# A two-layer transformer kernel: the MLP products by quarters with seven products in place of eight, and modulation weights summed along rows by VectorE

## What is computed

```python
h = modulate(rms_norm(x, mlp_norm[layer]), sh_m, sc_m)        # h * (1 + sc) + sh
x = x + gt_m * squared_relu_mlp(h, mlp_w1[layer], mlp_w2[layer])

def squared_relu_mlp(h, w1, w2):                              # w1: 1024 x 4096, w2: 4096 x 1024
    return jnp.square(jax.nn.relu(h @ w1)) @ w2

c_act = jax.nn.silu(c)                                        # 1024 values
mod = (c_act @ ada_w[layer] + ada_b[layer])                   # 1024 x 6144; kv_ada_w: 1024 x 2048
```

## Time and profile before

| | us |
|---|---|
| median of 3 runs | 2585.69 |
| lowest, highest | 2585.17, 2588.85 |
| the profiled execution | 2587.35 |
| its span, first to last instruction | 2585.6 |

### The profile page before, as it was taken

How to read it: one execution, slowest core, us unless ns; L and a number is a source line. 1 busy time by engine, 2 the same in 40 slices (tenths; PEclk the granted TensorE clock), 3 DMA queues, 4 the chain that set the end, 5 groups by cost and what they waited for, 6 DMA issues and landing times. The chain is left out here.

```text
span 2585.6 us, 22377 instructions
## 1 busy us (share of the span) xinstructions
PE 2444.9 (95%) x8264; PEld 1216.3 (47%) x8264; DVE 823.2 (32%) x1835; ACT 465.4 (18%) x995; POOL 42.9 (2%) x50
## 2 busy tenths in 40 slices
PE   6999899999999999989999999999999899998886
PEld 4444544444444645554444444464554643343332
DVE  4444432112122436653211213138642411110104
ACT  2232211110000324441211100021231200000001
POOL 0000000000000000000000000000000000000000
PEclk9999799999999999989999999999999899999998
DMA  8443213333433111112433433341003569999995
GB/s 341 158 168 147 98 65 130 130 130 130 169 157 130 57 65 50 49 74 98 163 130 132 172 151 130 130 163 65 33 1 130 230 266 427 426 426 425 424 422 205
DMA packets 45426, 452.29 MB, mean 175 GB/s; under 512 B 7784, under 2 KB 7784, under 8 KB 20240
## 3 DMA queue, kind: packets, MB, share of 16 engines
q1 hardware_dynamic: 37616, 435.64, 42.0%
q0 software_dynamic: 6528, 12.17, 1.3%
q10 hardware_dynamic: 1184, 3.19, 0.3%
HBM read 444.54 MB, written 18.39 MB: 179 GB/s over the span
## 5 line engine op out<-in xcount | busy, mean ns | idle before, releaser
L959 PE MATMUL ps<-big,ring 128*128 128x512 f32 x1024 | 448.9, 596 | 3.9 <-PEq L871 1.8
L901 PE MATMUL ps<-hT,ring 128*128 128x512 f32 x1024 | 444.3, 594 | 0.0
L959 PEld LDWEIGHTS ps<-big,ring 128*128 128x128 f32 x1024 | 192.6, 191 | 245.9 <-issue 245.9
L901 PEld LDWEIGHTS ps<-hT,ring 128*128 128x128 f32 x1024 | 193.9, 191 | 237.9 <-issue 236.6
L2572 PE MATMUL ps<-ring,big 128*64 128x512 f32 (+1 forms) x768 | 233.3, 614 | 25.2 <-issue 15.3
L512 PE MATMUL ps<-hT,ring 128*128 128x512 f32 x384 | 175.0, 607 | 2.1 <-ACT hT L429 2.1
L2572 PEld LDWEIGHTS ps<-ring,big 128*64 128x64 f32 (+1 forms) x768 | 85.2, 151 | 144.3 <-issue 131.0
L1653 PE MATMUL ps<-hT,ring 128*128 128x512 f32 x320 | 142.4, 600 | 2.7 <-DVE big L2035 1.7
L2572 PE MATMUL ps<-big 128*64 128x512 f32 (+1 forms) x352 | 130.0, 604 | 6.6 <-ACT big L2633 3.3
L207 DVE SCALAR_TENSOR_TENSOR tmp<-ring,cact,tmp 128x512 f32<-128x512 f32 (+1 forms) x192 | 131.6, 685 | 6.8
L856 DVE TENSOR_TENSOR mod<-ps,vec 128x4 f32 (+1 forms) x16 | 2.6, 162 | 367.4 <-PE ps L214 367.4
(11 more groups left out here) (433 smaller groups left out, 2506.6 us busy)
## 6 DMA issues: line engine op xcount, KB each, us to landing
ring<-in_stream SPq DMA_DIRECT2D x99, 2048.0 KB, 8.4
ring<-in_gate SPq DMA_DIRECT2D x17, 2048.0 KB, 29.2
ring<-in_up SPq DMA_DIRECT2D x16, 2048.0 KB, 25.2
ring<-in_down SPq DMA_DIRECT2D x15, 2048.0 KB, 27.4
big<-in_up SPq DMA_DIRECT2D x9, 2048.0 KB, 25.2
big<-in_down SPq DMA_DIRECT2D x8, 2048.0 KB, 27.1
big<-in_gate SPq DMA_DIRECT2D x7, 2048.0 KB, 24.8
hT<-in_down SPq DMA_DIRECT2D x5, 2048.0 KB, 26.5
```

What stands on the lines that cost most here:

```text
L901: last = pe.matmul(m.ps[:, j, :], w[:, k, j * P:(j + 1) * P], m.hT[:, k, :], start=(k == 0), stop=(k == KT - 1))
L959: last = pe.matmul(m.ps[:, bank(half, j), :], w[:, k, j * P:(j + 1) * P], hid[:, 8 * c + k, :], start=(c == 0 and k == 0), stop=(c == 3 an ...
```

## The change

**Products.** Rows and columns are split in half, and four products of quarters with their sums are made from seven products P1 to P7 (Strassen's scheme in Winograd's form). In the first product chunk 0 stays as it was; each of the other seven chunks is done in two pairs `(c, q)`. A pair makes four 128 x 256 quarters of hidden tiles f = 4c + q and g = 4c + 2 + q. The inner dimension is split into k = 0 to 3 and 4 to 7, so each P is 4 matmuls of 256 columns into its own bank (line L919 of the changed kernel). The sums of weight quarters (`sums_a`, `sums_b`) are made by VectorE ahead of the pair, those of `hT` (`t1`, `t2`, `t4`) once. VectorE joins the seven banks (`u2`, `u4`, `u3`, `c22`, `c11`, `c21`, `c12`), and ScalarE copies P1 out and applies ReLU and Square to each quarter. In the second product a step `s` is one `k` of one chunk with its partner `4 + k`: 32 steps (16 for each half of the output), each 7 products of 2 matmuls of 256 columns (L1108), accumulated over the 16 steps in seven banks. VectorE makes the weight sums and the sums of hidden quarters per step (`sums`: 8 additions of 256 in the first half, 7 in the second, where one sum of hidden quarters is left in place by the first half). `outputs` joins the banks after a half's last step and `joined` scales and adds to `xT` by quarters, so tiles come in the order 2, 3, 0, 1.

**Modulation.** The weights are laid out with outputs on partitions (`output_rows`, on the host, where the other weights are laid out too). The activated condition vector is spread over all partitions once per MLP (8 matmuls with the identity in place of 7 that kept TensorE busy, then a copy by ScalarE to `crow`). Each 128 outputs are one instruction over 1024 elements with an accumulator (L869), four (three in the second MLP) per chunk. The row sums by TensorE are gone. The first product's loop is unrolled.

TensorE, first product, the end of a chunk before, and the first pair and the beginning of the second after. `relu`, `h_ok`, `mm` are semaphores; L906 gives the slot back.

The diff, cut to the parts that the prediction speaks of:

```diff
+    def modulation(dve, n, j0, j1, o, done, total):
+        slot = n % RING
+        if j0 == 0:
+            dve.wait_ge(m.full[slot], 16 * (n // RING + 1))
+        for j in range(j0, min(j1, tiles)):
+            w = m.ring[:, slot, j * D:(j + 1) * D]
+            dve.scalar_tensor_tensor(w, w, 1.0, crow, ALU.mult, ALU.mult, accum_out=mod_out[:, o + j:o + j + 1]).then_inc(done, 1)
+        if j1 == 4:
+            dve.wait_ge(done, total)
+            dve.sem_inc(m.free[slot], 1)
...
+    bank = dict(P1=0, P6=1, P5=2, P7=3, P2=4, P4=5, P3=6)
+    b11, b12, b21, b22 = m.hT[:, 0:4, 0:H], m.hT[:, 0:4, H:T], m.hT[:, 4:8, 0:H], m.hT[:, 4:8, H:T]
+    pairs = [(c, q) for c in range(1, 8) for q in range(2)]
...
+                def product(name, a, b):
+                    out = m.ps[:, bank[name], 0:H]
+                    for k in range(4):
+                        ins = pe.matmul(out, a[:, k, :], b[:, k, :], start=(k == 0), stop=(k == 3))
+                    ins.then_inc(prod, 1)
...
+                pe.wait_ge(t_ok, 1)
+                pe.wait_ge(relu, 4)
+                pe.wait_ge(cond_ok, 1)
+                for i, (c, q) in enumerate(pairs):
+                    if q == 0:
+                        pe.wait_ge(m.full[chunk1(c)[0]], chunk1(c)[1])
+                    a11, a12, a21, a22 = quarters(c, q)
+                    if i:
+                        pe.wait_ge(p1_ok, i)
+                    product("P1", a11, b11)
+                    pe.wait_ge(s12_ok, i + 1)
+                    if i:
+                        pe.wait_ge(u2_ok, i)
+                    product("P6", s2, t2)
+                    if i:
+                        pe.wait_ge(u4_ok, i)
+                        pe.wait_ge(c22, i)
+                    product("P5", s1, t1)
+                    if i:
+                        pe.wait_ge(u3_ok, i)
+                    pe.wait_ge(s3_ok, i + 1)
+                    pe.wait_ge(t3_ok, 1)
+                    product("P7", a21, b12)
...
+                    product("P4", a22, t4)
+                    if i:
+                        pe.wait_ge(c12, i)
+                    pe.wait_ge(s4_ok, i + 1)
+                    product("P3", s4, b22)
+                    if q == 1:
+                        pe.wait_ge(prod, PRODUCTS * (i + 1))
+                        pe.sem_inc(m.free[chunk1(c)[0]], 1)
...
+                def sums_a(c, q):
+                    a11, a12, a21, a22 = quarters(c, q)
+                    if q == 0:
+                        dve.wait_ge(m.full[chunk1(c)[0]], chunk1(c)[1])
+                    c1.link(dve.tensor_tensor(s1, a21, a22, ALU.add))
+                    dve.tensor_tensor(s2, s1, a11, ALU.subtract).then_inc(s12_ok, 1)
+                    dve.tensor_tensor(a21, a11, a21, ALU.subtract).then_inc(s3_ok, 1)
+                def sums_b(c, q, i):
+                    dve.wait_ge(s12_ok, i + 1)
+                    dve.tensor_tensor(s4, quarters(c, q)[1], s2, ALU.subtract).then_inc(s4_ok, 1)
+                def ada(c, j0, j1):
+                    modulation(dve, at + 2 * c + 1, j0, j1, tiles * c, mod_done, tiles * (c + 1))
...
+                for i, (c, q) in enumerate(pairs):
+                    f, g = 4 * c + q, 4 * c + 2 + q
+                    ps = lambda name: m.ps[:, bank[name], 0:H]
+                    done = PRODUCTS * i
+                    dve.wait_ge(p1_ok, i + 1)
+                    dve.wait_ge(prod, done + 2)
+                    dve.tensor_tensor(u2, p1, ps("P6"), ALU.add).then_inc(u2_ok, 1)
+                    dve.wait_ge(u2_ok, i + 1)
+                    dve.wait_ge(prod, done + 3)
+                    dve.tensor_tensor(u4, u2, ps("P5"), ALU.add).then_inc(u4_ok, 1)
+                    dve.wait_ge(prod, done + 4)
+                    dve.tensor_tensor(u3, u2, ps("P7"), ALU.add).then_inc(u3_ok, 1)
+                    dve.wait_ge(u3_ok, i + 1)
+                    dve.tensor_tensor(hid[:, g, H:T], u3, ps("P5"), ALU.add).then_inc(c22, 1)
+                    if i + 1 < len(pairs):
+                        sums_a(*pairs[i + 1])
+                    dve.wait_ge(prod, done + 5)
+                    dve.tensor_tensor(hid[:, f, 0:H], p1, ps("P2"), ALU.add).then_inc(c11, 1)
+                    ada(c, 2 * q, 2 * q + 1)
+                    dve.wait_ge(prod, done + 6)
+                    dve.tensor_tensor(hid[:, g, 0:H], u3, ps("P4"), ALU.add).then_inc(c21, 1)
+                    dve.wait_ge(prod, done + 7)
+                    dve.wait_ge(u4_ok, i + 1)
+                    dve.tensor_tensor(hid[:, f, H:T], u4, ps("P3"), ALU.add).then_inc(c12, 1)
+                    if i + 1 < len(pairs):
+                        sums_b(*pairs[i + 1], i + 1)
+                    ada(c, 2 * q + 1, 2 * q + 2)
...
+                    def product(name, a, b):
+                        for q in range(2):
+                            ins = pe.matmul(m.ps[:, bank[name], q * H:(q + 1) * H], a[:, q * P:(q + 1) * P], b,
+                                            start=(first and q == 0), stop=(final and q == 1))
+                        ins.then_inc(prod, 1)
...
+                    product("P1", a11, b11)
+                    if s == 0:
+                        product("P2", a12, b21)
+                    if first and half:
+                        pe.wait_ge(u2_ok, 1)
+                    pe.wait_ge(st12_ok, s + 1)
+                    product("P6", s2, t2)
+                    if first and half:
+                        pe.wait_ge(u4_ok, 1)
+                        pe.wait_ge(c22_ok, 1)
+                    product("P5", s1, t1)
+                    if first and half:
+                        pe.wait_ge(u3_ok, 1)
+                    pe.wait_ge(st3_ok, s + 1)
...
+                    if s >= 2:
+                        dve.wait_ge(prod, PRODUCTS * (s - 1))
+                    c1.link(dve.tensor_tensor(s1, a21, a22, ALU.add))
+                    dve.tensor_tensor(s2, s1, a11, ALU.subtract).then_inc(chn, 1)
+                    c1.n += 1
+                    if half == 0:
+                        c1.link(dve.tensor_tensor(t1, b12, b11, ALU.subtract))
+                        dve.tensor_tensor(t2, b22, t1, ALU.subtract).then_inc(st12_ok, 1)
+                        dve.tensor_tensor(a21, a11, a21, ALU.subtract).then_inc(chn, 1)
+                        c1.n += 1
+                        dve.tensor_tensor(b12, b22, b12, ALU.subtract).then_inc(st3_ok, 1)
...
+                def joined(f, h):
+                    for q in range(2):
+                        x = m.xT[:, f + q, h * H:(h + 1) * H]
+                        ins = dve.scalar_tensor_tensor(x, cres[:, q * H:(q + 1) * H], gate[:, f + q:f + q + 1], x, ALU.mult, ALU.add)
+                        c1.n += 1
+                        ins.then_inc(chn, 1)
+                        if f % 4 == 2 and h == 0 or f % 4 == 0 and h == 1:
+                            dve.wait_ge(chn, c1.n)
+                            dve.sem_inc(added, 1)
+                    dve.wait_ge(chn, c1.n)
...
+                    dve.wait_ge(c22_ok, half + 1)
+                    joined(f + 2, 1)
+                    dve.wait_ge(prod, done + 5)
+                    dve.tensor_tensor(cres, v1, ps("P2"), ALU.add).then_inc(c11_ok, 1)
+                    dve.wait_ge(c11_ok, half + 1)
+                    joined(f, 0)
...
+                sums(0)
+                for s, (half, c, k) in enumerate(steps):
+                    if s + 1 < len(steps):
+                        sums(s + 1)
+                    i = 4 * half + c
+                    modulation(dve, at2 + 2 * i + 1, k, k + 1, tiles * (8 + i), mod_done, tiles * (i + 1))
+                    if half and c == 0 and k < 3:
+                        squares(k + 1)
+                    if c == 3 and k == 3:
+                        outputs(half)
+                for j in range(4, 7):
+                    squares(j)
...
+def output_rows(w, width=512):
+    w = np.asarray(w)
+    n = w.shape[1] // width
+    out = np.zeros((n, P, CH), w.dtype)
+    out[:, :, :width // P * D] = w.T.reshape(n, width // P, P, D).transpose(0, 2, 1, 3).reshape(n, P, width // P * D)
+    return out
```

More of the change, by code:

```diff
@@ L844, in phase_mlp @@
     tiles = width // P
[L845 to L857 removed]
+    crow = m.tmp[:, 0:D]
@@ new lines, in _ @@
+                ins.then_inc(cond_in, 1)
+                chunk, full, v = ring_chunk(m, at)
+                pe.wait_ge(full, v)
+                w = chunk.rearrange("p (k n) -> p k n", k=8)
+                for j in range(4):
+                    for k in range(KT):
+                        if j == 0:
+                            pe.wait_ge(h_ok, k + 1)
+                        last = pe.matmul(m.ps[:, j, :], w[:, k, j * P:(j + 1) * P], m.hT[:, k, :],
+                                         start=(k == 0), stop=(k == KT - 1))
+                    last.then_inc(mm, 1)
@@ new lines, in _ @@
+                for i, (c, q) in enumerate(pairs):
+                    f, g = 4 * c + q, 4 * c + 2 + q
+                    act.wait_ge(prod, PRODUCTS * i + 1)
```

(27 more changed lines are left out.)

263 lines of the change are left out of this document (149 added, 114 removed).

## The result

The changed kernel takes **2487.86 us** (median of 4 runs, 2485.9 to 2489.39) against 2585.94 (4 runs beside it): ratio 0.9618, 95% interval 0.9606 to 0.9629, 98 us less. The forecast was 2489, range 2477 to 2508. The profiled execution took 2489.1 us, its span 2487.2.

A forecast was written before the change was run, and what follows sets the result against it. The prediction took TensorE to bound the kernel, busy 2444.9 of 2585.6 us. Products -99.0, row sums -23.6 and late VectorE +25.3 gave -97.3 from 2587.35, or 2490.0, stated as 2489, range 2477 to 2508.

The forecast's parts named there:

- Products: Both MLPs' two products on TensorE: seven products of 256-column matmuls, 0.2158 us a record, replace eight: -99.0 us.
- Row sums: TensorE's modulation row sums in both products of both MLPs all go, the drain at chunk ends stays: -23.6 us.
- VectorE keeps up: VectorE's sums and modulations stay hidden: 4.9 us a second-product step against TensorE's 6.04, so they cost nothing.
- (a) to (d): VectorE late: ReLU before first pair +0.6, first product's end +0.6, second's start +0.4, its middle +1.9 us, both MLPs.
- (b) and (c): VectorE late at the first product's end, +0.3 us, and at the second product's start, +0.2 us, per MLP.
- (e): Second product's tail: row sums wait for VectorE's serial work, then run at 1.2 GHz: +8.7 and +11.4 us.
- (f): Second MLP's second product starts at 1.2 GHz after 2.8 us without TensorE work: +1.7 us, bound 0.
- 1: Rival: VectorE's accumulating modulation instruction takes twice its streaming time, 2.5 us in all: 2495 us; chance 0.14.
- 2: Rival: VectorE becomes the bound in the second product, 6.5 us a step, 0.43 over: 2507 us; chance 0.05.
- 3: Rival: the tails are cheaper, clock stays up and waits overlap, half of the 25 us: 2477 us; chance 0.08.
- 4: Rival: waits at product heads expose a 0.19 us weight load at each of 644 products: 2611 us; chance 0.03.
- 5: Rival: a 256-column record in the products costs 0.2258 us, giving 34 us back: 2522 us; chance 0.02.

The follow-up runs named there:

- first7: Kernel before with modulations by rows and the first product by seven products, the second by eight as before: 2513.98 us, ratio 0.9733.
- mods: Kernel before with only the modulation weights laid by output rows and summed by VectorE, both products still at eight: 2559.67 us, ratio 0.991.
- dose2: Changed kernel with two idle 128x512 additions on VectorE in 28 of the second product's 32 steps: 2488.45 us, ratio 0.9622.
- dose4: Changed kernel with four idle 128x512 additions on VectorE in 28 of the second product's 32 steps: 2537.07 us, ratio 0.9814.
- warm: Changed kernel with idle 128-column matmuls behind each MLP's last product, ahead of the row sums: 2480.06 us, ratio 0.9584.
- tail: Changed kernel with the last four blocks' squares in tiles of their own, summed block by block by TensorE: 2486.53 us, ratio 0.9619.
- combo: Changed kernel with both tail and warm ideas, sums against 128 columns of ones and fewer records in the second MLP: 2471.36 us, ratio 0.956.
- combo_major: As combo without idle matmuls, the second product's last two steps bank by bank and their modulations two steps earlier: 2463.82 us, ratio 0.9538.
- plain1024: Changed kernel with one more 128x1024 scalar_tensor_tensor without accumulator in 28 of the second product's 32 steps: 2486.36 us, ratio 0.962.
- split256: Kernel before with each 512-column matmul of the two products written as two of 256 columns: 2589.91 us, ratio 1.0024.

## Why the prediction was right, term by term

- **Products (-99.0).** Pace 0.216 us against 0.2158, 1568 + 1792 records as counted. `first7` against `mods` measures -23.8 and -24.8 for the first product (predicted -23.1 with +0.6 for its ends, and 1.4 for the ReLU waits of `mods`).
- **Row sums (-23.6).** Measured -23.3 by the ratio of the runs, -25.5 by stages. The first products gave 6.2 and 3.5 where I had 7.0 and 5.4, the second 8.8 and 7.0 where I had 6.5 and 4.7. The first two are short by the 1.4 us of ReLU waits each, but hold 1.1 us of clock: the first product of the first MLP starts at 1.2 GHz before (8 records in 4.50 us) and not in `mods` (3.44). 1.7 of the 8.8 is the start at full pace, which the changed kernel does not have, and 1.7 of the 7.0 is clock in the tail of the second MLP, whose one-column sums last 7.6 us before and 5.8 in `mods`. With the clock's 4.5 taken off and the waits' 2.8 put back, the row sums themselves are worth some 24: the term was right, and what came with it nearly cancelled.
- **VectorE keeps up.** A step takes 4.3 us, not 4.9, as 256-element additions follow each other every 0.34 and the modulation takes 1.22 + 0.08 in place of 1.37. `dose2` and `dose4` stand on either side of the edge.
- **(a) to (d).** (b) and (c), 0.5 us together, can't be told apart in the stage sums. TensorE's wait for the ReLU before pair 0: 0.73 against 0.40 (+0.3, as said). The middle of the first MLP: 0.67 + 1.06 = 1.7 against 1.6; of the second, 0.54 against 0.3.
- **(e) Tails (+8.7, +11.4).** From the last product's end to the next stage's first matmul: 785.33 to 802.16, 16.8 us, against 7.9 before; 1597.83 to 1623.67, 25.8, against 14.2. That is +8.9 and +11.7. The size came out closer than its parts: TensorE's sums start 8.1 and 9.7 us after the last product, where I had 7.2 and 9.3, and `warm` puts the clock's share at 1.5 and 3.9 (I had 2.1 and 2.4). In the second MLP I counted 24 records that run at 2.4 GHz before the change; it is 48, and 22 of them were at 1.2 GHz before too, from 1711.2 on, so that the sums last 10.2 us against 7.6, +2.6. That this meets my 2.4 is luck. The kernel before:

```profile
1710.13 1.26 PE L393 MATMUL ps<-ones,hT 128*128 128x1 f32 x10
1711.26 0.56 PE L393 MATMUL ps<-eps,hT 128*128 128x1 f32 x2
```

- **(f) (+1.7).** Did not come in the second MLP: its second product started at full pace after 1.71 us of idle time (1400.49, 8 records in 1.97). In the first MLP nine profiles share the code up to there and the same 3.08 us of idle time: it starts slow in five (both of the changed kernel, 8 records in 3.65 and 3.46, `warm`, `dose2`, `dose4`) and fast in four (`tail`, `combo`, `combo_major`, `plain1024`, in 1.97). So neither idle time nor the edit decides; what does stays open. The bound of 0 held.
- **Rivals.** 1 and the rule behind it: the accumulating instruction takes 1.218 us, as does the plain one beside it. The sentence of the Trainium skill (Vector Engine (DVE) Microarchitecture Reference, section 7) on half throughput does not hold for this instruction here, and the measurement decides. 2: `dose4` is that mechanism, made real; the room was 1.8 us a step. 3: the tails were not cheaper. 4: no load at a product's head is late. 5: `split256`.

By stages, predicted and measured: first MLP -29.5 and -30.1, -22.4 and -22.2; second MLP -27.9 and -28.3, -17.5 and -19.0. Only the last is over 1 us off, by (f). The stages together are 2.3 us better than foretold, and "between", which the change does not touch, gave 1.7 back. That 97.3 foretold meets 98.1 measured to within 1 us is therefore partly luck; that it is within 3 follows from the terms.

## What to carry to other kernels

When one engine is 95% busy and a second has room, moving a sum from the first to the second is free up to a number that can be worked out beforehand: the busy engine's step less the other's (here 6.05 less 4.3). The price shows at the ends, where the pipeline runs out: there the second engine's serial chain is exposed (9 and 12 us of the 123 that went), and what followed on the idle engine ran at 1.2 GHz here. Two causes in series must be taken away together: in the first MLP's tail the clock alone brought 1.5 us, the additions alone 1.3, both 5.1; in both tails `warm` brought 5.4, `tail` nothing and `combo`, which also sums with fewer records, 15.4.
